# Hybrid DeltaNet / neighbourhood-attention layer: three levels of the triangular inverse as column-group products turned back by transposes

## The reference, cut to what matters

```
lmat = jnp.where(strict, jnp.einsum('nbhid,nbhjd->nbhij', kb, k) * decay, 0.0)
tinv = lax.linalg.triangular_solve(lmat + eye, jnp.broadcast_to(eye, lmat.shape),
                                   left_side=True, lower=True, unit_diagonal=True)
u = tinv @ (v * beta[..., None])
w = tinv @ (kb * jnp.exp(gc)[..., None])
...
v_new = u_i - w_i @ s
o_i = qg_i @ s + a_i @ v_new
s = s * gl_i + jnp.swapaxes(kd_i, -1, -2) @ v_new
```

## Time and profile before

| | us |
|---|---|
| median of three runs | 1555.48 (1549.24 to 1555.66) |
| the profiled execution | 1549.53 |
| its span | 1547.8 |
| PE busy | 1476.8 (95%) |
| ACT busy | 598.5 (39%) |
| DVE busy | 715.6 (46%) |

### The profile page before, as it was taken

The page is one execution under the profiler, slowest core; times in us unless marked ns, Lnnn a source line. Parts: engine busy times, 40 slices in busy tenths (PEclk is TensorE's granted clock), DMA queues, the critical chain, the costliest instruction groups (busy, mean ns, idle before and its releaser), DMA issues. The chain is left out here.

```text
span 1547.8 us, 26292 instructions
## 1 busy us (share of the span) xinstructions
PE 1476.8 (95%) x10544; PEld 1407.3 (91%) x10544; DVE 715.6 (46%) x1511; ACT 598.5 (39%) x1291; POOL 118.8 (8%) x112
## 2 busy tenths in 40 slices
PE   6799999999999999999998998998999999999998
PEld 3689899989999998999986887997999999999998
DVE  2555655655464565656345654645332322232321
ACT  4653625435261534437155554325222211222211
POOL 0011020202001020200031221000000000000000
PEclk9799999999999999999999999999999999999999
DMA  8452323133233314213325211620222321222322
GB/s 311 143 142 81 95 83 102 56 90 97 81 98 86 101 51 125 62 54 107 124 62 187 60 42 42 205 79 28 82 68 81 89 75 55 81 68 81 89 63 80
DMA packets 202262, 143.22 MB, mean 93 GB/s; under 512 B 9471, under 2 KB 187687, under 8 KB 201911
## 3 DMA queue, kind: packets, MB, share of 16 engines
q1 hardware_dynamic: 202167, 141.91, 30.8%
HBM read 125.85 MB, written 16.42 MB: 92 GB/s over the span
## 5 line engine op out<-in xcount | busy, mean ns | idle before, releaser
L1400 PE MATMUL ps<-h_part,w_part 128*128 128x320 f32 x2112 | 312.3, 310 | 7.9 <-DVE h_part L2426 5.6
L1400 PEld LDWEIGHTS ps<-h_part,w_part 128*128 128x128 f32 x2112 | 311.6, 189 | 8.3 <-issue 8.3
L990 PE MATMUL ps<-hT_r,WAH_r 128*128 128x320 f32 x960 | 235.2, 326 | 15.6 <-DVE P6c L2138 5.5
L990 PE MATMUL ps<-xT_r,WAH_r 128*128 128x320 f32 x960 | 218.7, 309 | 0.0
L990 PEld LDWEIGHTS ps<-hT_r,WAH_r 128*128 128x128 f32 x960 | 155.2, 190 | 26.9 <-ACT raws L1502 9.9
L990 PEld LDWEIGHTS ps<-xT_r,WAH_r 128*128 128x128 f32 x960 | 160.8, 188 | 0.0
L1400 PE MATMUL ps<-a_part,w_part 128*128 128x320 f32 x1056 | 156.7, 309 | 1.3 <-DVE w_part L2401 1.3
L1400 PEld LDWEIGHTS ps<-a_part,w_part 128*128 128x128 f32 x1056 | 155.0, 188 | 1.8 <-issue 1.8
L2401 DVE TENSOR_TENSOR w_part<-oT,w_part 128x1024 fp32r<-128x1024 f32 (+1 forms) x60 | 79.9, 1332 | 127.0 <-ACT w_part L1888 126.3
L990 PE MATMUL ps<-hT_r,W_r 128*128 128x320 f32 x576 | 131.2, 309 | 0.0
L1888 ACT ACTIVATE w_part<-oT 128x1024 fp32r<-128x1024 f32 (+1 forms) x60 | 68.4, 1141 | 85.7 <-PE ps L1400 71.9
(11 more groups left out here) (328 smaller groups left out, 2363.6 us busy)
## 6 DMA issues: line engine op xcount, KB each, us to landing
oT<-in_ffn_w SPq DMA_DIRECT2D x44, 512.0 KB, 3.8
WAH<-in_w_ada SPq DMA_DIRECT2D x20, 1024.0 KB, 6.9
W<-in_w_in SPq DMA_DIRECT2D x36, 512.0 KB, 4.3
naT<-in_w_in SPq DMA_DIRECT2D x24, 512.0 KB, 4.1
oT<-in_ffn_w SPq DMA_DIRECT2D x16, 704.0 KB, 4.8
ext_dram<-naT SPq DMA_DIRECT2D x28, 320.0 KB, 4.1
GCB<-gc_dram SPq DMA_DIRECT2D x8, 640.0 KB, 4.3
W<-in_w_pa SPq DMA_DIRECT2D x8, 512.0 KB, 4.3
```

The source lines that it names most:

```text
L990: m = e.matmul(ps[:, b, 0:n], w[:, k, :], x[:, k, a:a + n], start=k == 0 and i == 0, stop=k == KD - 1 and i == 2, skip_group_check=True)
L1400: m = e.matmul(ps[:, bank + b, 0:w], w_part[wp][:, s, k, :], x_part[xp][:, k, a:a + w], start=k == 0 and n == 0, stop=k == k_n - 1 and n = ...
```

## The change

The six products of n = 3, 4, 5 exchange their operands. The compact operand (128 rows, 32 columns) is now stationary, on one of four column groups (unit u on group u mod 4, output partitions 32 (u mod 4) and up), and the 128x128 tile moves. The result is transposed: PSUM bank 5 holds 32 x 128 of each unit, four units above one another and three such sets side by side (the third with two units, 64 partitions). ACT copies it to `across` (a part of the tile `V`, which is free by then) with two activations, and PE turns it with three transposes into bank 6, in the layout from which DVE and ACT read as before. The other PE work stays; `before` has a gap of its own for each turn, and the numbers of blocks are dealt out anew. On ACT the six new copies and `strip_out` (the former `extra_out` and `raw_out`) stand in a new order. P6 and Y6 take the two directions by turns.

```diff
-                before = dict(zip(("P3", "Y3", "P4", "Y4", "P5", "Y5", "P6", "Y6", "scan", "first"), {
-                    "first": (5, 3, 3, 3, 2, 2, 2, 2, 1, 1),
-                    "mid": (5, 3, 4, 4, 4, 4, 4, 2, 1, 1),
-                    "last": (8, 4, 4, 4, 4, 4, 4, 4, 2, 2)}[part]))
+                gaps = ("P3", "turn P3", "Y3", "turn Y3", "P4", "turn P4", "Y4", "turn Y4", "P5", "turn P5", "Y5", "turn Y5", "P6", "Y6", "scan", "first")
+                before = dict(zip(gaps, {
+                    "first": (5, 1, 2, 1, 2, 1, 1, 1, 2, 1, 1, 1, 2, 1, 1, 1),
+                    "mid": (5, 1, 2, 1, 3, 1, 2, 2, 2, 1, 2, 1, 4, 2, 1, 2),
+                    "last": (7, 1, 2, 1, 2, 1, 2, 2, 2, 1, 2, 1, 4, 4, 4, 4)}[part]))
...
+                def wide(name, one, other):
+
+                    for u in range(U):
+                        g, r = 32 * (u % 4), u // 4 * P
+                        m = e.matmul(ps[g:g + 32, 5, r:r + P], one[:, u, :], other[:, u, :], start=True, stop=True, skip_group_check=True)
+                    pe_dn.done(m, f"{name} wide")
+
+                def turn_wide(name):
+
+                    for r in range(3):
+                        n = min(4, U - 4 * r) * 32
+                        m = e.transpose(ps[:, 6, r * P:r * P + n], across[0:n, r, :], sq_c[0:n, ID, 0:n])
+                    pe_dn.done(m, name)
...
-                    for u in range(U):
-                        m = e.matmul(ps[:, 5, u * 32:(u + 1) * 32], (LNTd if n < 5 else LNTp)[:, u, :], Xc[:, u, :], start=True, stop=True, skip_group_check=True)
-                    pe_dn.done(m, f"P{n}")
+                    wide(f"P{n}", Xc, LNTd if n < 5 else LNTp)
+                    filler(fill, before[f"turn P{n}"])
+                    wait(act_dn, f"P{n}" if n < 5 else "P5 wide")
+                    turn_wide(f"P{n}")
...
-                for u in range(U):
+                for u in (t + d * NT for t in range(NT) for d in range(2)):
...
+                def wide_out(name, done):
+
+                    wait(pe_dn, f"{name} wide")
+                    e.activation(across[:, 0:2, :], ps[:, 5, 0:2 * P].rearrange("p (r c) -> p r c", r=2), ACT.Copy)
+                    act_dn.done(e.activation(across[0:64, 2, :], ps[0:64, 5, 2 * P:3 * P], ACT.Copy), done)
...
+                wide_out("P3", "P3")
+                strip_out(0)
+                big("3")
+                wide_out("Y3", "Y3")
+                wide_out("P4", "P4")
+                wide_out("Y4", "Y4")
+                strip_out(1)
+                big("4")
+                wide_out("P5", "P5 wide")
                 wait(pe_dn, "P5")
-                act_dn.done(e.activation(Pc[:, :, :], ps[:, 5, 0:U * 32].rearrange("p (u c) -> p u c", u=U), ACT.Copy), "P5")
-                if part == "mid":
-                    extra_out(1, h)
-                big("5")
+                act_dn.done(e.activation(Pc[:, :, :], ps[:, 6, 0:U * 32].rearrange("p (u c) -> p u c", u=U), ACT.Copy), "P5")
+                wide_out("Y5", "Y5 wide")
                 wait(pe_dn, "Y5")
                 act_dn.done(e.activation(Yc[:, :, :], ps[:, 6, 0:U * 32].rearrange("p (u c) -> p u c", u=U), ACT.Copy), "Y5")
+                strip_out(2)
+                big("5")
```

More of the change, by code:

```diff
@@ L118, in pe_steps @@
     for n in (3, 4, 5):
-        names += [f"P{n}", f"Y{n}"]
+        names += [f"P{n} wide", f"P{n}", f"Y{n} wide", f"Y{n}"]
     names += ["ada half", "P6", "Y6"]
@@ L129, in act_steps @@
 def act_steps():
-    names = ["kq", "hi 1", "L32", "L diag", "L pairs", "hi 2", "kd", "hi 3", "hi 4", "P5", "hi 5", "Y5", "ada half", "hi z", "P6", "Y6"]
+    names = ["kq", "hi 1", "L32", "L diag", "L pairs", "hi 2", "kd", "P3", "hi 3", "Y3", "P4", "Y4", "hi 4", "P5 wide", "P5", "Y5 wide", "Y5", "hi 5", "ada half", "hi z", "P6", "Y6"]
     for s in range(NT):
@@ L495, in build @@
         Yc = sb("Yc", [P, U, 32], dn)
+        across = V[:, :, :].rearrange("p u c -> p (u c)")[:, 0:3 * P].rearrange("p (r c) -> p r c", r=3)
         P6c = sb("P6c", [P, NT, 64], dn)
@@ L1134, in head @@
                         wait(act_dn, "P5")
-                    for u in range(U):
-                        m = e.matmul(ps[:, 6, u * 32:(u + 1) * 32], XTd[:, u, :], Pc[:, u, :], start=True, stop=True, skip_group_check=True)
-                    pe_dn.done(m, f"Y{n}")
+                    wide(f"Y{n}", Pc, XTd)
+                    filler(fill, before[f"turn Y{n}"])
+                    wait(act_dn, f"Y{n}" if n < 5 else "Y5 wide")
+                    turn_wide(f"Y{n}")
                 pe_dn.done(ada_rows(4, 2 * P, WA, ld_wa[0:1], h * 16 + 16), "ada half")
@@ L1653, in head, with strip_out @@
                 act_dn.done(m, "kd")
-                if part == "mid":
[L1655 to L1661, removed]
-                    extra_out(1, h)
[L1663 to L1669, removed]
+                def wide_out(name, done):
+                    wait(pe_dn, f"{name} wide")
+                    e.activation(across[:, 0:2, :], ps[:, 5, 0:2 * P].rearrange("p (r c) -> p r c", r=2), ACT.Copy)
+                    act_dn.done(e.activation(across[0:64, 2, :], ps[0:64, 5, 2 * P:3 * P], ACT.Copy), done)
+                def strip_out(n):
+                    kind = STRIPS[part][1 + n]
+                    if kind == "k":
+                        raw_out("k", h + 2)
+                    elif kind != "v":
+                        extra_out(kind, h)
+                wide_out("P3", "P3")
[7 more added lines that the diff above has]
+                wide_out("P5", "P5 wide")
                 wait(pe_dn, "P5")
-                act_dn.done(e.activation(Pc[:, :, :], ps[:, 5, 0:U * 32].rearrange("p (u c) -> p u c", u=U), ACT.Copy), "P5")
-                if part == "mid":
-                    extra_out(1, h)
-                big("5")
+                act_dn.done(e.activation(Pc[:, :, :], ps[:, 6, 0:U * 32].rearrange("p (u c) -> p u c", u=U), ACT.Copy), "P5")
+                wide_out("Y5", "Y5 wide")
                 wait(pe_dn, "Y5")
                 act_dn.done(e.activation(Yc[:, :, :], ps[:, 6, 0:U * 32].rearrange("p (u c) -> p u c", u=U), ACT.Copy), "Y5")
+                strip_out(2)
+                big("5")
                 wait(pe_dn, "ada half")
@@ L2155, in head @@
                     mask = lv_c[:, 2 * (n - 3):2 * (n - 3) + 2, :].unsqueeze(2).to_broadcast([P, 2, NT, 32])
-                    done(e.tensor_tensor(pc4, ps[:, 5, 0:U * 32].rearrange("p (d t c) -> p d t c", d=2, t=NT), mask, ALU.mult), f"P{n}")
+                    done(e.tensor_tensor(pc4, ps[:, 6, 0:U * 32].rearrange("p (d t c) -> p d t c", d=2, t=NT), mask, ALU.mult), f"P{n}")
                     wait(pe_dn, f"Y{n}")
```

## The result

The changed kernel takes 1578.16 us (median of 4 runs, 1575.13 to 1579.54), the kernel before in the same comparison 1552.5 us (median of 4, 1549.24 to 1555.66). The ratio is 1.0163, with a 95% interval of 1.013 to 1.0196: slower by 1.6%. The span of the profiled execution is 1575.1 us, against 1547.8 before: +27.3 us. The prediction was 1572 us, 1554 to 1590.

The account below looks back on a forecast made before the run. PE was taken to bound the kernel: own work -34 us, but with the hand-over waits +12 us at full clock, plus 8 us of slow clock, makes +20 us. Forecast 1572 us, between two bases; range 1554 to 1590.

Parts of the forecast that it names:

- What bounds the kernel: Whole kernel: PE, busy 1476.8 of 1547.8 us, so its work counts as long as nothing makes it wait.
- PE's own work: Wide products, turns, P6 and Y6: -4.3 us a head, -34 us in eight heads.
- The hand-overs in a mid head: PE waits on ACT's copies: 6.25 us against 4.3 saved, +1.95 us a mid head, +11.7 in six.
- The stall at the turn of Y3: Mid heads: PE waits 3.95 us because Y3's copy queues behind `big("3")` and its DMA; range 3.6 to 5.3.
- the two boundaries: Ends of strips k and 1 in mid heads: the new strip waits 1.1 us each for ACT's copy-out.
- The clock: Half clock behind the stall in six mid heads: 1.3 us each, +8 us, bounds 0 and 18.
- rival 2: Mid-head stall comes without a fall of the clock: +12 us, 1561 to 1567 us; chance 0.20.
- Head 0 and head 7: First and last head: waits of about 4.2 and 4.6 us, net -0.1 and +0.3 us.
- The sum: Whole kernel: +12 us at full clock, +8 for the clock, together +20 us.
- The saved PE time arrives: Rival: Y3's copy doesn't wait for the DMA; mid heads gain 2.0 us each, 1538 to 1544 us; chance 0.11.
- The column groups don't keep pace: Rival: each wide product 0.65 us longer, 31 us over 48, about 1600 us; chance 0.10.
- Gain and waits cancel: Rival: own work at its better end, DMA at 3.7 us, no clock: 1553 to 1559 us; chance 0.06.

Follow-up runs that it names:

- the wait alone: Kernel before, plus only a PE wait for `big("3")` one block behind Y3 in six mid heads: 1577.27 us, ratio 1.0153.
- the full turns: Changed kernel with Y3's copy ahead of `big("3")`, plus the third transpose of each turn on all 128 partitions: 1527.02 us, ratio 0.9845.
- the copy moved ahead: Changed kernel with ACT's copy of Y3 put ahead of `big("3")` and its DMA wait, in all heads: 1540.33 us, ratio 0.991.
- the filled stall: Changed kernel plus 22 throwaway matmuls of 320 columns on PE ahead of the turn of Y3 in mid heads: 1564.9 us, ratio 1.0082.
- the boundaries moved: Changed kernel, mid heads' strips ending right ahead of product Y4 and the turn of Y5, copied out first: 1565.4 us, ratio 1.0087.
- the quadrants by turns: Kernel before with only P6's and Y6's matmuls taking the two directions by turns: 1546.15 us, ratio 0.9952.

## Why the prediction was right, and where it was off

**What bounds the kernel.** Right. PE is the engine without gaps, and each microsecond that it waits is lost: the wait alone, in the kernel before, costs more than its own length.

**PE's own work.** Right to about a tenth of a microsecond a step. The rows of head 2:

```profile
289.39 0.46 PE L991 MATMUL ps<-hT_r,naT_r 128*128 128x320 f32 x2
289.78 0.85 PE L1128 MATMUL ps<-tri,Xc 128*32 128x128 f32 x20
...
290.95 0.46 PE L991 MATMUL ps<-xT_r,WAH_r 128*128 128x320 f32 x2
291.25 0.46 PE L991 MATMUL ps<-hT_r,naT_r 128*128 128x320 f32 x2
291.55 0.58 PE L1135 MATMUL ps<-sq_c,V 128*128 128x128 f32 x3
...
292.45 0.46 PE L991 MATMUL ps<-xT_r,WAH_r 128*128 128x320 f32 x2
```

The product is 290.95 - 289.39 - 0.58 = 0.98 us (predicted 0.99), the turn 292.45 - 291.25 - 0.58 = 0.62 (0.67). P6 takes 0.94 (1.34 less 0.4):

```profile
327.37 0.46 PE L991 MATMUL ps<-hT_r,W_r 128*128 128x320 f32 x2
327.76 0.80 PE L1162 MATMUL ps<-X,tri 64*64 64x64 f32 x20
...
328.89 0.45 PE L991 MATMUL ps<-xT_r,WAH_r 128*128 128x320 f32 x2
```

In a head that is 6 x (2.24 - 0.98 - 0.62) + 2 x 0.4 = 4.6 us saved, where I said 4.3. Reading the four-group price off line 967 at 256 columns, and the change of layout off two other places, was enough; the full turns then showed the second of these terms by itself, 0.29 us. The Trainium skill's 62 ns a matmul in one decoding mode ("TensorE: Matmul & The Clock Gate", "Step-by-step: what each phase is for") isn't what bounds these twenty: they take 0.85 us with the tail, 0.043 us each.

**The hand-overs in a mid head.** Right in place and size. The stall at the turn of Y3 was 3.95 predicted and is 3.91; the two boundaries were 1.1 each and are 1.08 and about 1.0 (its wait shows as 0.85 and more); the first block behind Y3 waits 0.2 us for `extra_out(0)`, where I said 0.1. Against 4.6 us saved, the waits of 6.2 us leave +1.6 us a mid head (predicted +1.95). In head 6 the stall is 1.3 us longer, by the late landing; 5.24 us is inside the 3.6 to 5.3 that I gave. Two of the runs take these waits out one at a time: the copy moved ahead gains the stall with the clock on top, and the boundaries gain about their size.

The Trainium skill ("TensorEngine Tiling (Array Packing)", "PSUM Bottleneck") warns that after a fourfold speed-up of TensorE the copies out of PSUM may become the bottleneck. By their length they aren't it here: ACT is busy 39% of the span. The same copy of Y3, of 0.37 and 0.26 us, costs 5.5 us or more in a mid head in one order and no wait on PE in the other.

**The clock.** Here one term was mis-sized. I took 1.3 us for each mid head, for one slow stretch of 3.3 us part of which would fall into the stall. In four of the six heads nothing of it does: in head 2 the granted clock is still 1.00 at 299.80, it is 0.50 from 300.7, when PE is at full work, and the whole stretch is paid, 1.7 us. In heads 1 and 6 a part does, 2.0 and 0.2 us, but the stretch is 6.8 us long, and half of what is left is 2.4 and 3.3 us. Together that is 12.6 us, 2.1 a mid head, instead of 8; the filled stall gave 1.9. With this term the sum comes out: 6 x 1.6 + 1.3 + 12.6 = 23.5 us against the measured 22.8.

My lower bound of that term, none at all, rested on the wait of 2.1 us at 947.4 in the earlier trace rows behind which the clock stayed. It was one row, and the same trace has another that says the opposite, 30 us later:

```profile
977.20:979.10 1.90, 0.00 (x1) 0.00 (x0) 1.86 (x4) 0.57 (x1) 0.00 (x0) 1.00 0.31 58
979.50:982.80 3.30, 3.30 (x14) 3.30 (x13) 3.07 (x6) 1.97 (x3) 0.00 (x0) 0.50 0.59 185
```

The wait at 947.4 itself recurs in all ten traces with the same 2.12 us, and in seven of them the clock is halved at or behind it, in three (the kernel before among them) it isn't. The six waits of 2.0 to 2.3 us added to the kernel before were all followed by half clock; but the changed kernel has one in head 0, ahead of P3's turn, that is as long and wasn't, for the clock stays at 1.00 until 205.1:

```profile
120.28 0.64 PE L1135 MATMUL ps<-sq_c,V 128*128 128x128 f32 x3 [2.21 <-ACT V L1676]
```

So the length of the wait alone doesn't say whether a wait of 2 us costs clock; what decides it no run here isolates. At the stalls of 3.4 us and more ahead of the turn of Y3 the clock fell in all twelve cases, six in this kernel and six in the one with the boundaries moved. So for rival 2, the stall without the clock, 0.20 was too much. A single wait that goes unpunished is no bound for the next.

**Head 0 and head 7.** Head 0 came out at -0.9 us for -0.1 predicted; the wait ahead of P3's turn was named at 2.4 us and is 2.2. Head 7 was +0.3 predicted and +2.7 measured, up to the merge's first product. The wait of Y6 for ACT's copy of P6 was named at 2.5 us and is 2.46 (below it a stretch, with the granted clock of 0.50 behind the busy times):

```profile
792.69 1.33 PE L1170 MATMUL ps<-XT,P6c 64*64 64x64 f32 x20 [2.46 <-ACT P6c L1709]
793.95 0.90 PE L991 MATMUL ps<-hT_r,WAH_r 128*128 128x320 f32 x2
```

```profile
795.00:799.00 4.00, 4.00 (x17) 4.00 (x16) 0.81 (x1) 0.00 (x0) 3.18 (x1) 0.50 0.27 58
```

What I left out is that this wait, too, costs clock: 0.50 for 6.8 us, from half a microsecond before PE goes on, which is about 3 us. The step that was off is the same as above, a wait below 3.3 us taken as free of it.

**The sum.** Forecast +20 us on the span, measured +27.3. The missing 7 us: mid heads +3.1 (22.8 for 19.7; the clock is some 4.6 us more than I took, waits and work some 1.5 us less), head 7 +2.4, head 0 -0.8, and 2.7 us outside the heads, which the forecast had at nothing. Of these, 2.0 lie behind the merge's start; there the slow stretch that begins at 825.9 in the earlier trace rows is 6.8 us long in this trace (from 850.2) instead of 3.4, which is 1.7 us. Why it is longer stays open. The 0.7 us ahead of the first R say nothing of the change: nothing differs up to there, and the first R stands at 109.6 in the kernel before, at 111.1 with the quadrants by turns and at 109.2 with the wait alone, though all three run the same code until then. Head 0's own difference is of that size too: the filled stall has the changed kernel's head 0 word for word, and there it is 1.6 us shorter.

**The rivals.** *The saved PE time arrives* didn't happen, but its price was right: with the stall out of the way, by the copy moved ahead, a mid head gains 2.2 us where it said 2.0, and the kernel takes 1540 us where it said 1538 to 1544. *The column groups don't keep pace* fell with the product's 0.98 us. *Gain and waits cancel* would have needed no fall of the clock.

## What to carry to other kernels

When an edit gives an engine's in-order queue a new job that a full engine waits for, look at what stands ahead of it in that queue. A step that waits for a DMA costs nothing as long as nobody is behind it, and here it turned a gain of 13 us into a loss of 26; two lines in another order brought it back. Count a wait on PE as its length plus the slow clock at its end, which here nearly doubled six waits of 2 us and added half to those of 4; after other waits of 2 us it didn't fall, so take such a price as likely, not as sure. And a product that is cheap because its operands changed places pays for each change of the array's layout, 0.3 us there and back: do the odd-shaped last piece in the shape of the others, if its surplus rows harm nobody. Where the next product changes the layout anyway, that gave only 0.1.

## What the runs showed of the hardware

- At a wait of PE of 2.0 to 2.3 us the granted clock fell to 0.50 in six cases of six (the wait alone), for 3.4 us or more each; a wait of 2.12 us that all ten traces have was followed by it in seven, and one of 2.21 us in the changed kernel (at 120.28) wasn't. The slow stretch began between 2.0 us before PE went on and 1.05 us after, over the twelve waits in mid heads of these two kernels. The 22 throwaway products in the stall kept the clock at 1.00 in all six mid heads.
- Three transposes of 128x128 between blocks take 0.33 us; with the third on 64 rows they take 0.62 us, though it has half the rows. Ahead of a product that changes the layout anyway the difference was 0.09 us.
- Twenty 64x64 matmuls of two quadrants take 0.94 us when the quadrants alternate and 1.34 us when ten of one are followed by ten of the other.
- Twenty matmuls with a 32-column stationary operand on four column groups, 128 columns each, take 0.98 us between blocks. The same products with the operands in each other's places, on the whole array with 32 columns, take 2.24 us.
